# Two transformer blocks on one core: where the weights and the upper tiles begin, modulo 128 bytes

## The chip, the cores and the metric

The kernel runs on 1 of the 8 cores of a Trainium2 chip. The metric is the device time of one execution in microseconds, lower is better. The core has a matrix engine (TensorE, PE in the profile, its weight loads PEld), three engines for elementwise work (VectorE is DVE, ScalarE is ACT, GpSimd is POOL) and a queue for transfers (SyncE, SP). They share the on-chip memory SBUF (128 partitions, tiles are columns of bytes in each) and are ordered by semaphores that the kernel sets by hand. Matrix products go to the eight banks of PSUM (`ps`).

## The reference

A sequence of 512 tokens, 1024 wide, float32, passes through three layers. Cut to the order of the work:

```python
for i in range(2):                               # first block: NSA mixer, then sliding-window mixer
    mod = silu(c) @ ada_w[i] + ada_b[i]          # six vectors: sh1, sc1, g1, sh2, sc2, g2
    h = rms_norm(x, g) * (1 + sc1) + sh1
    y = nsa_mixer(h, ...) if i == 0 else swa_sink_mixer(h, ...)
    x = x + (1 + g1) * rms_norm(y, g)
    h = rms_norm(x, g) * (1 + sc2) + sh2
    y = relu(h @ w_up) ** 2 @ w_down             # 1024 -> 4096 -> 1024
    x = x + (1 + g2) * rms_norm(y, g)
x = x + hybrid_mixer(rms_norm(x), ...)           # second block: pooling and gated linear attention
x = x + memory_cross_attention(rms_norm(x), rms_norm(mem), wq, wkv, wo)
x = x + conv_ffn(rms_norm(x), ...)               # 1024 -> 2 x 2816 -> 1024
return rms_norm(x)
```

All matrix products are float32.

## The kernel before

**Products.** Every weight matrix is cut into units of 1024 x 128 elements (DC = 8 blocks of 128 x 128), 309 units in all, in one order of use. A unit is loaded by SP into a ring of four slots, `raw`. ScalarE rounds it to the fast float type of TensorE, `wh` (line 2540), and POOL writes the remainder, `wl = raw - wh` (line 802). The activations are split in the same way into a high and a low half: `ah`/`al`, `hh`/`hl`, `fh`/`fl`, `oh`/`ol`, `mh`/`ml`, `xoh`/`xol`. A float32 product is then three fast ones for each of the 8 blocks (lines 909, 910, 911 in `products`): `wh` by high, `wl` by high, `wh` by low. In these the weights are the stationary operand (128 columns) and the activations the moving one (512 tokens). `gemm_first` (lines 972, 973, 977) does the same for the first three units of a stage, block by block; `chunks` (1030 to 1032) for a part of a unit. `gemm_pairs` (957 to 959) and `last_values` (1510 to 1512) turn the roles around: 128 tokens of the activations are stationary and two units of weights move (2 x 128 columns); `compress` (1313 to 1315) as well, with 124 stationary columns that step by 496 bytes. For the 256 tokens of the memory the moving operand `mh` has 256 columns.

**Stages.** nsa_in (43 to 172 us in the trace), attention of NSA (to 349), nsa_out (to 404), mlp0 (to 774), swa_in (to 840), sliding-window attention (to 900), swa_out and mlp1 (to 1309), mix_in with pooling and gated linear attention (to 1449), mix_out and the products of the memory (to 1529), cross attention (to 1614), xo (to 1660), ffn (to the end). In the MLPs blocks of eight units alternate: up on `ah`, down on `hh`. In ffn up takes `fh`, down takes `hh`.

**Order.** Each engine runs its own program, written out by hand. TensorE waits for `lo_done` (POOL's wl) before a unit and for `evac` (the bank has been read); ScalarE may overwrite a slot of `wh` when TensorE has done with it (`unit_used`); SP loads into `raw` when POOL has done with the slot.

**Places.** `at(name, kib, shape)` puts a tile at `sb0 + kib * 1024` bytes of each partition. `sb0` is the first free byte rounded up to 64; here it is 16512, a multiple of 128. The lower tiles have whole KiB: `x` 0, `ah` 16, `al` 32, `y` 48 (also `xol`, `pr`, `me`), `raw` 64, `wh` 80, `wl` 96, then `rs`, `tt`, `sq` and the table of small inputs `sm` at 126, whose columns are listed in SMALL (2689 of them). Behind the table lie small tiles, `ident_r` and `mask_r` (the identity and two masks for the attention scores, made by the copies of lines 1799 to 1801 from columns of the table), and from `w0` on the upper region, which the stages use in turn: `hh` at w0, `hl` w0 + 16, `fh` w0 + 48, `fl` w0 + 32, `oh` w0, `ol` w0 + 38, `mh` w0 + 16, `ml` w0 + 24, `xoh` w0 + 50, `qs`, `ks`, `vv`, `pt` and others, each at w0 plus a multiple of 128 bytes. The table's 10756 bytes end at s1 = 126 + 169/16 KiB, and w0 = s1 + 3 KiB = 139.5625 KiB, which is 64 bytes past a multiple of 128.

Of the kernel before, what the change touches and what calls it, by code (L numbers as in the profile page):

```python
# [7 lines left out]
F32R = mybir.dt.float32r  # L8
# [5 lines left out]
P = 128  # L14
D = 1024
S = 512
DC = D // P
SC = S // P
# [6 lines left out]
KB = 1024  # L25
NEG = -1.0e30
RING = 4


UNITS_NSA_IN = 21  # L30
# [16 lines left out]
for _name, _count in STAGES:  # L47
# [2 lines left out]
UNITS = _n  # L50


SMALL = (("ones", P), ("ident", P), ("diag", P), ("prev", P), ("cmp_add", SC * P),
         ("inv", 1), ("cT", DC), ("ada_b", 96), ("norm_g", 64), ("pe", 32), ("b1", 4), ("b2k", 1), ("b2v", HD),
         ("w2", 4 * HD), ("sinks", HEADS), ("norm_mix", DC), ("norm_xattn", DC), ("norm_mem", DC),
         ("norm_ffn", DC), ("norm_final", DC), ("pool_scale", 4), ("gk_b", 2), ("gla_norm", 1),
# [2 lines left out]
COL = {}  # L59
_n = 0  # L60
for _name, _count in SMALL:
    COL[_name] = (_n, _n + _count)
    _n += _count
SMALL_COLS = _n
# [174 lines left out]
def over_units(eng, a, b, one):  # L239

    while a < b and (a % RING or b - a < 2 * RING):
        one(a, a % RING)
        a += 1
    turns = max(0, (b - a) // RING)
    if turns > 0:
        with eng.Fori(0, turns) as it:
            for slot in range(RING):
                one(it * RING + (a + slot), slot)
    for u in range(a + turns * RING, b):
        one(u, u % RING)  # L250


def build(nc, src, out):
# [4 lines left out]
    def at(name, kib, shape, dt=F32):  # L258

        return nc.alloc_sbuf_tensor_at(name, shape, dt, offset=sb0 + int(kib * KB))  # L260
# [12 lines left out]
    al = at("al", 32, [P, DC, S], F32R)  # L273
    y = at("y", 48, [P, DC, S])
    raw = at("raw", 64, [P, RING, DC, P])
    wh = at("wh", 80, [P, RING, DC, P], F32R)
    wl = at("wl", 96, [P, RING, DC, P], F32R)
    rs = at("rs", 112, [P, 2, S])
    tt = at("tt", 116, [P, 3, S])
    sq = at("sq", 122, [P, 2, S])  # L280
    sm = at("sm", 126, [P, SMALL_COLS])
    s1 = 126 + (SMALL_COLS * 4 + 63) // 64 / 16
    sxx = at("sxx", s1, [P, P])
    k1 = s1 + 0.5
    mod = at("mod", k1, [P, 96])
# [3 lines left out]
    warm = at("warm", k1 + 0.90625, [P, 1])  # L289
    neg_sinks = at("neg_sinks", k1 + 0.9375, [P, HEADS])  # L290
    ident_r = at("ident_r", k1 + 1, [P, P], F32R)
    mask_r = at("mask_r", k1 + 1.5, [P, 2, P], F32R)
    w0 = k1 + 2.5
    assert w0 + 68 <= 207.75, w0

    def small(name):
# [16 lines left out]


    pair = at("pair", w0, [P, 4, S])
    acc_in = at("acc_in", 112, [P, 1024])
    rot_h = at("rot_h", w0 + 12, [P, 2, 2, S], F32R)
    rot_l = at("rot_l", w0 + 20, [P, 2, 2, S], F32R)
    vv = at("vv", w0 + 28, [P, 2, SC, 4 * HD])
    pair_c = at("pair_c", 48, [P, 4, S])  # L320
    vtmp = at("vtmp", w0 + 36, [P, 2, S])
    ada_in2 = at("ada_in2", 116, [P, 2, 1024])
    xb_h = [at(f"xb_h{i}", (w0 + 44, 48)[i], [P, 16, 4 * NCMP], F32R) for i in range(2)]
    xb_l = [at(f"xb_l{i}", (w0 + 52, w0 + 36)[i], [P, 16, 4 * NCMP], F32R) for i in range(2)]
    hp = at("hp", 124, [P, 2, 2 * P])
    gate_t = at("gate_t", 56, [P, S])
    v_t = at("v_t", w0 + 44, [P, S])
    h1 = at("h1", w0 + 60, [P, 2, 2, 4 * NCMP])
# [8 lines left out]
    x2 = at("x2", 48, [P, 2, 4, S])  # L337
    ang = at("ang", 48, [P, 6, S])
    pos_i = at("pos_i", 60, [P, S], I32)
    trig = at("trig", 112, [P, 2, S])  # L340

    qs = at("qs", w0 + 16, [P, 4, S], F32R)
    ks = at("ks", w0 + 8, [P, 2, 2, S], F32R)
# [2611 lines left out]
def lay_out(i):  # L2955
# [24 lines left out]
    for what, n in (("u", 0), ("u", 1), ("d", 0), ("u", 2), ("d", 1), ("d", 2)):  # L2980
# [28 lines left out]
        quarter=np.arange(P)[:, None] == 32 * np.arange(4)[None, :], invcnt=np.broadcast_to(counts, (P, 64)), tri=np.where(np.arange(P)[:, None] % 64 <= np.arange(HD)[None, :], 1.0, 0.0))  # L3009
    table = np.concatenate([np.asarray(parts[name], dtype=f) for name, _ in SMALL], axis=1)  # L3010
    assert table.shape == (P, SMALL_COLS)
# [23 lines left out]
```

## Time and profile before

| | us |
|---|---|
| median of three runs | 2047.81 |
| all runs | 2047.92, 2042.06, 2047.81 |
| span of the profiled execution | 2041.0 |
| TensorE busy | 1973.7 (97%) |
| its weight loads | 1617.8 (79%) |
| VectorE busy | 1131.7 (55%) |
| POOL busy | 945.6 (46%) |
| ScalarE busy | 701.7 (34%) |

The span runs from the first to the last instruction of one profiled execution. That execution's own time is not given beside it; the runs lie 1 to 7 us above the span. Matmuls overlap their neighbours in the pipeline, so that a busy share of TensorE or the mean duration of a matmul doesn't say how fast they follow each other; the starts do.

### The profile page before, as it was taken

The numbers are of one execution on the slowest core, as the hardware profiler recorded it, in microseconds if no ns is written. First come the engines' busy times: TensorE is split into PE (matmuls) and PEld (weight loads), VectorE is DVE, ScalarE is ACT, GpSimd is POOL, SyncE is SP. The second block draws the span as 40 slices with busy tenths as digits, with TensorE's granted clock in tenths as the row PEclk, the third lists the DMA queues.
The fourth block names the chain that finished last, engine by engine and source line by source line (L and its number), as shares of the span: only waits on it lengthen the run. The fifth ranks groups of instructions, "written<-read, shape, count | busy, mean of one in ns | idle before, by whom it ended". The sixth has DMA issues, their size and how long they took to land.

```text
span 2041.0 us, 27018 instructions
## 1 busy us (share of the span) xinstructions
PE 1973.7 (97%) x10293; PEld 1617.8 (79%) x10293; DVE 1131.7 (55%) x1747; ACT 701.7 (34%) x1225; POOL 945.6 (46%) x552
## 2 busy tenths in 40 slices
PE   6998999999999999999999999999999999999997
PEld 5888777778888887877888888788797788888885
DVE  7675775973545567766322314686453368345163
ACT  3353654432222233654222213342443342222222
POOL 1465553465444445554544444542373244444442
PEclk9998999999999999999999999999999999999998
DMA  7765331545555524721332233221342223333331
GB/s 290 240 216 165 113 102 48 200 163 188 195 176 196 170 68 130 207 88 52 114 98 99 93 96 101 63 83 63 103 145 83 71 70 118 93 93 99 97 93 62
DMA packets 79989, 252.22 MB, mean 124 GB/s; under 512 B 12160, under 2 KB 12672, under 8 KB 79616
## 3 DMA queue, kind: packets, MB, share of 16 engines
q1 hardware_dynamic: 79872, 250.61, 38.0%
q8 instruction: 79, 1.29, 0.3%
q14 instruction: 38, 0.31, 0.0%
HBM read 235.21 MB, written 15.37 MB: 123 GB/s over the span
## 4 chain that ended last, share of the span: by engine, by line
PE 73%; issue 12%; POOL 7%; DVE 5%; ACT 3%; POOLq 0%; DVEq 0%; ACTq 0%
PE ps L909 20%; PE ps L911 20%; PE ps L910 20%; POOL wl L802 6%; PE ps L1195 2%; PE ps L1135 2%; ACT pr L2687 2%; PE ps L1167 1%; PE ps L1472 1%; DVE st L1947 1%; PE ps L1497 1%; POOL al L858 1%; PE ps L977 1%; POOL x L850 1%; PE ps L957 0%
## 5 line engine op out<-in xcount | busy, mean ns | idle before, releaser
L802 POOL TENSOR_TENSOR wl<-raw,wh 128x1024 fp32r<-128x1024 f32 x309 | 770.9, 2501 | 946.9 <-ACT wh L2540 946.7
L2540 ACT CAST wh<-raw 128x1024 fp32r<-128x1024 f32 x309 | 322.3, 1050 | 905.7 <-PE ps L911 840.5
L909 PE MATMUL ps<-ah,wh 128*128 128x512 f32 x904 | 357.7, 396 | 1.5 <-DVE pair L1877 1.5
L910 PE MATMUL ps<-ah,wl 128*128 128x512 f32 x904 | 352.8, 390 | 0.0
L911 PE MATMUL ps<-al,wh 128*128 128x512 f32 x904 | 352.6, 390 | 0.0
L909 PE MATMUL ps<-hh,wh 128*128 128x512 f32 x688 | 270.7, 393 | 1.9 <-DVE hl L2488 1.7
L911 PE MATMUL ps<-hl,wh 128*128 128x512 f32 x688 | 270.3, 393 | 0.0
L910 PE MATMUL ps<-hh,wl 128*128 128x512 f32 x688 | 268.0, 390 | 0.0
L909 PEld LDWEIGHTS ps<-ah,wh 128*128 128x128 f32 x904 | 170.1, 188 | 40.2 <-issue 2.6
L910 PEld LDWEIGHTS ps<-ah,wl 128*128 128x128 f32 x904 | 170.2, 188 | 36.3 <-issue 1.5
L911 PEld LDWEIGHTS ps<-al,wh 128*128 128x128 f32 x904 | 170.1, 188 | 36.0
L909 PEld LDWEIGHTS ps<-hh,wh 128*128 128x128 f32 x688 | 129.3, 188 | 30.5 <-DVE hl L2488 3.2
L910 PEld LDWEIGHTS ps<-hh,wl 128*128 128x128 f32 x688 | 129.2, 188 | 28.9
L911 PEld LDWEIGHTS ps<-hl,wh 128*128 128x128 f32 x688 | 129.2, 188 | 28.7
L911 PE MATMUL ps<-fl,wh 128*128 128x512 f32 x328 | 129.0, 393 | 0.0
L910 PE MATMUL ps<-fh,wl 128*128 128x512 f32 x328 | 128.2, 391 | 0.0
L909 PE MATMUL ps<-fh,wh 128*128 128x512 f32 x328 | 127.9, 390 | 0.0
L2687 ACT ACTIVATE pr<-ps,st 128x512 f32<-128x512 f32 (+1 forms) x192 | 94.2, 504 | 56.0 <-DVE st L1947 46.0
L2109 DVE TENSOR_SCALAR rs<-ps 128x512 f32<-128x512 f32 x64 | 44.2, 690 | 114.9 <-PE ps L911 109.9
L821 POOL TENSOR_SCALAR pr<-pr,st,gates 128x512 f32<-128x512 f32 (+3 forms) x128 | 81.5, 654 | 56.4 <-DVE st L1975 56.2
L1135 PE MATMUL ps<-ks,qs 128*128 128x256 f32 (+3 forms) x384 | 88.4, 336 | 5.7 <-ACT pr L2687 3.7
L2122 DVE TENSOR_TENSOR y<-ps,y 128x512 f32<-128x512 f32 x32 | 22.1, 691 | 127.3 <-PE ps L911 127.3
(402 smaller groups left out, 3262.7 us busy)
## 6 DMA issues: line engine op xcount, KB each, us to landing
raw<-in_units SPq DMA_DIRECT2D x309, 512.0 KB, 3.5
ada_mlp<-in_ada SPq DMA_DIRECT2D x64, 512.0 KB, 3.6
ada<-in_ada SPq DMA_DIRECT2D x16, 512.0 KB, 15.7
qs<-qscr SPq DMA_DIRECT2D x32, 256.0 KB, 3.4
ada_in<-in_ada SPq DMA_DIRECT2D x16, 512.0 KB, 3.6
ks<-kscr SPq DMA_DIRECT2D x24, 256.0 KB, 4.4
x<-in_xT SPq DMA_DIRECT2D x1, 2048.0 KB, 13.5
qscr<-rot_h SPq DMA_DIRECT2D x16, 128.0 KB, 2.4
```

What stands on the lines that cost most here:

```text
L802: nc.gpsimd.tensor_tensor(wl[:, slot], raw[:, slot], wh[:, slot].bitcast(F32), ALU.subtract).then_inc(lo_done, 1)
L821: op = nc.gpsimd.tensor_scalar(o, o, st[:, 2, n % 4, i:i + 1], gates[:, i, c:c + 1], ALU.mult, ALU.mult)
L850: nc.gpsimd.tensor_tensor(x[:, c], y[:, c], x[:, c], ALU.add).then_inc(x_new_pool, 1)
L909: nc.tensor.matmul(out_ap, wh[:, slot, k], high[:, k0 + k], start=first and k == 0, stop=False)
L910: nc.tensor.matmul(out_ap, wl[:, slot, k], high[:, k0 + k], start=False, stop=False)
L911: mm = nc.tensor.matmul(out_ap, wh[:, slot, k], low[:, k0 + k], start=False, stop=last and k == ks - 1)
L1135: nc.tensor.matmul(o, qs[:, Q_SLOT[j], i * P:(i + 1) * P], ks[:, slot, part, k0 * P:k1 * P], start=part == 0, stop=False)
L1195: mm = nc.tensor.matmul(ps[HD * h:HD * h + HD, bank, q[0] * P:(q[-1] + 1) * P], vv[:, kind, kb, col_v:col_v + HD], pt[:, n[h] % 4, place[k ...
L2109: link(v.tensor_scalar(rs[:, k % 2], b, 0.0, None, ALU.max))
L2122: v.tensor_tensor(y[:, c], bank(), y[:, c], ALU.add).then_inc(evac, 1)
L2540: a.copy(wh[:, slot], raw[:, slot]).then_inc(hi_done, 1)
L2687: a.activation(pr[:, n % 3, b * S + col:b * S + col + width], ps[:, plan.s_bank(w, b), col:col + width], ACT.Exp, bias=shift[:, i:i + 1], ...
```

## The change

It moves tiles and does nothing else. PAD is 1/8 KiB, 128 bytes. `wh` and `wl` begin 64 bytes later (PAD / 2), `rs` to `sm` and the tiles behind them 128 bytes later. `mask_r` no longer has a tile of its own: it lies over the columns prev and diag of the table, from which it is made, and the two columns change places in SMALL so that their order is that of `mask_r`. That frees 1 KiB, and w0 becomes 139, a multiple of 128 bytes. So `wh` and `wl` go from 0 to 64 modulo 128, all that is placed from w0 goes from 64 to 0, `mask_r` from 64 to 0; `ah`, `al`, `y`, `raw`, `xol`, the table keep 0, and `ident_r` and `sxx` keep 64.

```diff
--- before.py
+++ after.py
@@ -25,6 +25,7 @@
 KB = 1024
 NEG = -1.0e30
 RING = 4
+PAD = 1 / 8
 
 
 UNITS_NSA_IN = 21
@@ -50,7 +51,7 @@
 UNITS = _n
 
 
-SMALL = (("ones", P), ("ident", P), ("diag", P), ("prev", P), ("cmp_add", SC * P),
+SMALL = (("ones", P), ("ident", P), ("prev", P), ("diag", P), ("cmp_add", SC * P),
          ("inv", 1), ("cT", DC), ("ada_b", 96), ("norm_g", 64), ("pe", 32), ("b1", 4), ("b2k", 1), ("b2v", HD),
          ("w2", 4 * HD), ("sinks", HEADS), ("norm_mix", DC), ("norm_xattn", DC), ("norm_mem", DC),
          ("norm_ffn", DC), ("norm_final", DC), ("pool_scale", 4), ("gk_b", 2), ("gla_norm", 1),
@@ -273,13 +274,13 @@
     al = at("al", 32, [P, DC, S], F32R)
     y = at("y", 48, [P, DC, S])
     raw = at("raw", 64, [P, RING, DC, P])
-    wh = at("wh", 80, [P, RING, DC, P], F32R)
-    wl = at("wl", 96, [P, RING, DC, P], F32R)
-    rs = at("rs", 112, [P, 2, S])
-    tt = at("tt", 116, [P, 3, S])
-    sq = at("sq", 122, [P, 2, S])
-    sm = at("sm", 126, [P, SMALL_COLS])
-    s1 = 126 + (SMALL_COLS * 4 + 63) // 64 / 16
+    wh = at("wh", 80 + PAD / 2, [P, RING, DC, P], F32R)
+    wl = at("wl", 96 + PAD / 2, [P, RING, DC, P], F32R)
+    rs = at("rs", 112 + PAD, [P, 2, S])
+    tt = at("tt", 116 + PAD, [P, 3, S])
+    sq = at("sq", 122 + PAD, [P, 2, S])
+    sm = at("sm", 126 + PAD, [P, SMALL_COLS])
+    s1 = 126 + PAD + (SMALL_COLS * 4 + 63) // 64 / 16
     sxx = at("sxx", s1, [P, P])
     k1 = s1 + 0.5
     mod = at("mod", k1, [P, 96])
@@ -289,8 +290,9 @@
     warm = at("warm", k1 + 0.90625, [P, 1])
     neg_sinks = at("neg_sinks", k1 + 0.9375, [P, HEADS])
     ident_r = at("ident_r", k1 + 1, [P, P], F32R)
-    mask_r = at("mask_r", k1 + 1.5, [P, 2, P], F32R)
-    w0 = k1 + 2.5
+    mask_r = at("mask_r", 126 + PAD + COL["prev"][0] / 256, [P, 2, P], F32R)
+    w0 = 139
+    assert k1 + 1.5 <= w0
     assert w0 + 68 <= 207.75, w0
 
     def small(name):
@@ -313,16 +315,16 @@
 
 
     pair = at("pair", w0, [P, 4, S])
-    acc_in = at("acc_in", 112, [P, 1024])
+    acc_in = at("acc_in", 112 + PAD, [P, 1024])
     rot_h = at("rot_h", w0 + 12, [P, 2, 2, S], F32R)
     rot_l = at("rot_l", w0 + 20, [P, 2, 2, S], F32R)
     vv = at("vv", w0 + 28, [P, 2, SC, 4 * HD])
     pair_c = at("pair_c", 48, [P, 4, S])
     vtmp = at("vtmp", w0 + 36, [P, 2, S])
-    ada_in2 = at("ada_in2", 116, [P, 2, 1024])
+    ada_in2 = at("ada_in2", 116 + PAD, [P, 2, 1024])
     xb_h = [at(f"xb_h{i}", (w0 + 44, 48)[i], [P, 16, 4 * NCMP], F32R) for i in range(2)]
     xb_l = [at(f"xb_l{i}", (w0 + 52, w0 + 36)[i], [P, 16, 4 * NCMP], F32R) for i in range(2)]
-    hp = at("hp", 124, [P, 2, 2 * P])
+    hp = at("hp", 124 + PAD, [P, 2, 2 * P])
     gate_t = at("gate_t", 56, [P, S])
     v_t = at("v_t", w0 + 44, [P, S])
     h1 = at("h1", w0 + 60, [P, 2, 2, 4 * NCMP])
@@ -337,7 +339,7 @@
     x2 = at("x2", 48, [P, 2, 4, S])
     ang = at("ang", 48, [P, 6, S])
     pos_i = at("pos_i", 60, [P, S], I32)
-    trig = at("trig", 112, [P, 2, S])
+    trig = at("trig", 112 + PAD, [P, 2, S])
 
     qs = at("qs", w0 + 16, [P, 4, S], F32R)
     ks = at("ks", w0 + 8, [P, 2, 2, S], F32R)
```

## Rows read from the trace of the kernel before

**Rows 1.** The page, busy us (share) xinstructions; granted clock in tenths over 40 slices

```profile
PE 1973.7 (97%) x10293; PEld 1617.8 (79%) x10293; DVE 1131.7 (55%) x1747; ACT 701.7 (34%) x1225; POOL 945.6 (46%) x552
...
PEclk9998999999999999999999999999999999999998
```

**Rows 2.** The chain that ended last, shares of the span by line

```profile
by line: PE ps L909 20.1%; PE ps L911 20.1%; PE ps L910 19.9%; issue 12.1%; POOL wl L802 5.5%; PE ps L1195 2.1%; PE ps L1135 1.9%; ACT pr L2687 1.6%; PE ps L1167 1.5%; PE ps L1472 0.8%; DVE st L1947 0.8%; PE ps L1497 0.7%; POOL al L858 0.6%
```

**Rows 3.** The page, costliest groups: xcount | busy us, mean ns | idle before

```profile
L802 POOL TENSOR_TENSOR wl<-raw,wh 128x1024 fp32r<-128x1024 f32 x309 | 770.9, 2501 | 946.9 <-ACT wh L2540 946.7
...
L909 PE MATMUL ps<-ah,wh 128*128 128x512 f32 x904 | 357.7, 396 | 1.5 <-DVE pair L1877 1.5
...
L909 PE MATMUL ps<-hh,wh 128*128 128x512 f32 x688 | 270.7, 393 | 1.9 <-DVE hl L2488 1.7
...
L909 PE MATMUL ps<-fh,wh 128*128 128x512 f32 x328 | 127.9, 390 | 0.0
```

**Rows 4.** Line 909, two stretches on ah: ns min/median/max, first to last start us

```profile
L909 PE MATMUL ps<-ah,wh x40: 389/389/389, 423.4 to 449.9; 128*128 128x512 f32 x40
...
L909 PE MATMUL ps<-ah,wh x64: 389/389/397, 1125.9 to 1168.8; 128*128 128x512 f32 x64
```

**Rows 5.** The same view, stretches on hh and on fh

```profile
L909 PE MATMUL ps<-hh,wh x63: 394/394/394, 1170.2 to 1212.7; 128*128 128x512 f32 x63
...
L909 PE MATMUL ps<-fh,wh x128: 388/388/388, 1793.8 to 1881.0; 128*128 128x512 f32 x128
```

**Rows 6.** The same view, a stretch on xoh

```profile
L909 PE MATMUL ps<-xoh,wh x43: 397/397/398, 1629.8 to 1659.2; 128*128 128x512 f32 x43
```

**Rows 7.** The timeline of TensorE, three triples on ah: start us, us, instruction

```profile
149.75 0.28 PE L957 MATMUL ps<-wh,ah 128*128 128x256 f32 x1
...
150.83 0.28 PE L957 MATMUL ps<-wh,ah 128*128 128x256 f32 x1
```

**Rows 8.** The timeline, three triples with mh moving

```profile
1501.80 0.28 PE L909 MATMUL ps<-mh,wh 128*128 128x256 f32 x1
...
1502.86 0.28 PE L909 MATMUL ps<-mh,wh 128*128 128x256 f32 x1
```

**Rows 9.** Lines 957 and 1510, mh as the weights: stretches, and three triples of each state

```profile
L957 PE MATMUL ps<-wh,mh x32: 276/276/286, 1508.9 to 1519.4; 128*128 128x256 f32 x32
...
1511.94 0.28 PE L957 MATMUL ps<-wh,mh 128*128 128x256 f32 x1
...
1512.96 0.28 PE L957 MATMUL ps<-wh,mh 128*128 128x256 f32 x1
...
L957 PE MATMUL ps<-wh,mh x16: 281/281/388, 1520.5 to 1525.9; 128*128 128x256 f32 x16
...
1523.80 0.28 PE L957 MATMUL ps<-wh,mh 128*128 128x256 f32 x1
...
1524.86 0.28 PE L957 MATMUL ps<-wh,mh 128*128 128x256 f32 x1
...
L1510 PE MATMUL ps<-wh,mh x7: 276/276/276, 1603.0 to 1605.1; 128*128 128x256 f32 x7
...
L1510 PE MATMUL ps<-wh,mh x7: 276/276/285, 1607.9 to 1610.0; 128*128 128x256 f32 x7
```

**Rows 10.** The groups of TensorE by shape: other products of 512 columns

```profile
L972 PE MATMUL ps<-ah,wh 128*128 128x512 f32 x144 | 58.5, 407 | 9.9 <-ACT ah L2599 7.3 <-ACT ah L2597 2.6
...
L909 PE MATMUL ps<-oh,wh 128*128 128x512 f32 x64 | 25.6, 400 | 0.7 <-DVE ol L2361 0.7
```

**Rows 11.** The chain in order of time, in nsa_in: start us, us, what

```profile
84.98 2.50 POOL wl L802
```

**Rows 12.** The span by windows: us, busy us (xinstructions) of each engine, PEclk, DMA, GB/s

```profile
900.00:1309.00 409.00, 405.58 (x1893) 332.45 (x1891) 151.72 (x224) 122.67 (x154) 188.11 (x82) 1.00 0.29 92
```

**Rows 13.** The groups of POOL by shape, the same subtraction into al and fl

```profile
L858 POOL TENSOR_TENSOR al<-y,ah 128x512 fp32r<-128x512 f32 x12 | 15.5, 1291 | 13.1 <-ACT y L2604 10.1 <-ACT ah L2597 3.0
...
L858 POOL TENSOR_TENSOR fl<-y,fh 128x512 fp32r<-128x512 f32 x3 | 3.9, 1298 | 4.9 <-ACT fh L2597 4.9
```

## The prediction

> **What bounds the kernel now.** I read the page first: the busy table says that TensorE works for 97% of a span of 2041.0 us, and the slices that it does so at a granted clock of mostly 9 to 10 tenths (2.4 GHz) [rows 1]. No other engine passes 55%. The chain of work that ended last puts 60% of the span on three lines, 909 to 911 [rows 2]. They are the three products of one step (k) of a matrix product: wh by the high half of the activations, wl by the same, wh by the low half. I call these three a triple. So the question is how fast triples follow each other.
>
> The mean durations of the groups (390 ns) can't tell that, since matmuls are pipelined [rows 3]. The starts can. The view of one line in a stretch gives its count with the first and the last start, so a pitch is (last - first)/(count - 1). Where do the tiles stand, modulo 128 bytes? Before, the lower tiles (ah, al, wh, wl) stand at 0, everything from w0 on (hh, hl, fh, fl, oh, ol, mh, ml, xoh) at 64, xol at 0 again. That sorts the same instruction into classes; W is the weights' (stationary) remainder, M that of the moving operand:
> - 512 columns, W0/M0 (ah): (1168.8 - 1125.9)/63 = 681 ns a triple, in another stretch 26.5/39 = 679.5; I take 680 [rows 4].
> - 512 columns, W0/M64: hh (1212.7 - 1170.2)/62 = 685.5; fh, the longest stretch, 87.2/127 = 686.6; I take 686.7 [rows 5].
> - 512 columns, W0 with a moving operand that changes between 64 and 0 (xoh, xol): 29.4/42 = 700 [rows 6].
> - 256 columns, W0/M0 (ah as weights, wh moving): 1.08/3 = 360 in the timeline [rows 7].
> - 256 columns, W0/M64 (mh moving): 1.06/3 = 353 [rows 8].
> - 256 columns, W64/M0 (mh as weights, wh moving): 10.5/31 = 339 over 32 triples, 1.02/3 = 340 in the timeline; but the 16 triples that follow on the same line, after a wait, keep 1.06/3 = 353. Their matmuls last 281 ns each, those of the 32 last 276; both stretches of line 1510, the same class, have 276, so the first state [rows 9].
>
> Shape, clock and engine are the same inside each size, so the start of the operands in memory is what is left. All exceed the bare streaming of the columns (3 x 512/2.4 = 640 ns, 320 ns for 256): W0/M0 by 40 at both sizes, W64/M0 by 20, or by 33 when it has settled in its second state.
>
> **The change, part by part.** After it the weights wh, wl stand at 64 and every other large tile at 0 (the assertion on w0 allows it: w0 = 139 KiB). All main triples become W64/M0. These are relative places: were the base itself 64 off, the class with weights in the shifted region and the moving operand in the lower one would still be that of rows 9.
>
> The program has 1056 triples on ah (904 on line 909, 144 in gemm_first, 8 in chunks), 1080 on hh, fh and oh (688 + 328 + 64), 64 on xoh (eight units of eight) [rows 3, 10]. 216 of those on ah belong to nsa_in and mix_in, where TensorE also waits for the POOL's wl, for gates and for scans; in the chain from 64 us on POOL wl stands with some 2.5 us for each unit [rows 11]. Half of their gain counts, so 1056 becomes 948. The rest is a stream with TensorE alone on the path: in the mlp stage of 900 to 1309 us it is busy 405.58 of 409 us [rows 12].
>
> With X as the triple at W64/M0 and 512 columns, the change of the time is 948 x (X - 680) + 1080 x (X - 686.7) + 64 x (X - 700) ns = 2092 X - 1431.1 us. Break-even is X = 684 ns.
>
> X itself is in no row: no 512-column product has W64/M0. From W0/M0 I see that 256 more columns for each matmul cost exactly their streaming, 320 ns a triple [rows 4, 7]; so 340 becomes 660, and the second state, 353.3, becomes 673.3. At W0/M64 the same step costs 333 (353.3 to 686.7), which would put 340 at 673 too. Of four entries into W64/M0 three settled at 340 (the first pair stretch and both of line 1510) and one at 353 [rows 9]. I take three streams at 660 and one at 673.3: X = 663.3, and 2092 x 0.6633 - 1431.1 = -43.4 us.
>
> Smaller terms: mh with 256 columns moving, 64 triples from 353 to about 343, -0.6 us. gemm_pairs on ah, 128 triples from 360 to the 353 of W0/M64, -0.9, half hidden: -0.4. gemm_pairs and line 1510 on mh become W0/M64, 64 triples from 343 to 353: +0.6. compress (32 triples): its weights step by 496 bytes, so they meet all remainders before and after: nothing.
>
> Attention: qs, ks, mask_r, vv, pt go from 64 to 0, ident_r stays. Lines 1195 and 1135 hold 4.0% of the chain, 82 us [rows 2]; a pitch that moved by 5% either way, the spread of rows 4 to 6 being 3%, gives at most 4 us, and I take 0.
>
> The other engines: POOL's subtraction takes 1291 ns into al at 0 and 1298 into fl at 64 [rows 13], so wl at 64 costs under 1% of 2.5 us; POOL is idle 947 us before it [rows 3], and ScalarE, which writes wh, is busy 34% of the span [rows 1]. That cover stays while a unit of eight triples takes 5.3 us against POOL's 2.5. The DMAs of raw don't move; a unit of 512 KB each 5.3 us is 99 GB/s beside 92 now over the mlp stage [rows 12]. mask_r now lies over prev and diag, which nobody reads afterwards: the same two copies in setup. The swap of diag and prev moves columns in one table: nothing.
>
> Sum: -43.4 - 0.6 - 0.4 + 0.6 = -43.8 us. The profiled span is 2041.0; the runs show 2042.06 to 2047.92, so 1 to 7 us lie around it; the page names no own time for the profiled execution. The sum is taken from the median, 2047.8: **2004 us**.
>
> One rule speaks against it. The Trainium skill, "SBUF — State Buffer", section "Who interferes with whom", says that TensorE has two independent read ports, one for the moving operand and one for weights, and never waits on anyone; where a tile starts would then change nothing, the rival of no effect below. The classes at 680, 686.7 and 700 ns [rows 4 to 6] contradict it here. The same skill, "TensorE: Matmul & The Clock Gate", section "Back-to-back issue gap", gives N/2.4 + 2.5 ns for one matmul, 647.5 ns a triple; by that as X the estimate would be 2092 x 0.6475 - 1431.1 = -77 us. The best class here stands 20 ns above bare streaming for three, not 7.5, so no row bears it out.
>
> **Rivals.**
> 1. All in the first state: X = 660 gives -50.2, about 1997 us. For it: three of four entries, 32 triples in a row.
> 2. All in the second, or an added column costs as at M64: X = 673.3 gives -22.5, about 2025 us. For it: the one entry after a stall; every block of the MLP is such an entry.
> 3. No effect: alignment isn't the cause, but the stage or what runs beside it: 2048. Against: hh and ah alternate in one stage, each block with its own pitch [rows 4, 5].
> 4. Slower: the offset weights cost at 512 columns what an offset moving operand does, or what the mixed class does. Its place is each switch from one matmul to the next, where the next weights are fetched beside the moving columns; X lies between 686.7 and 700, say 693, and gives +18.7, about 2066 us. It decides from X = 687 on (+0.3%). Against: rows 9, where W64 is the fastest class; for it: only 256 columns are shown there.
>
> **How the numbers follow.** Mixed states as forecast 0.45, rival 1 0.17, rival 2 0.18, rival 3 0.08, rival 4 0.07, and 0.05 for something that I don't see. Range: down to rival 1 with all of the discounted 216 triples (2.2), 4 us in attention and 4 of the runs' own spread, 1987; up to rival 2 with 4 us: 2030. That leaves out rivals 3 and 4 and the rest. A measurement of this kernel tells about 0.3% (6 us) from no change. Faster 0.83, same 0.09, slower 0.08.
>
> **What would show it.** In the profile after: the starts of line 909 on ah and on hh must have one and the same pitch, 660 or 673; equal at 680 or above means that the step from 256 to 512 columns was wrong. xoh must fall from 700 to that value, the pair triples on mh rise from 340 to about 353. The spans of the mlp stages must shrink by 2.5 to 3.5%, attention hardly; if attention moves by over 4 us, that term was wrong. The 2.5 us of POOL's wl must stay; if TensorE's idle time grows by waits for it, the cover was thinner than I said. A pitch in which 660 appears, with a time that hasn't fallen, would mean that something else had bound the streams.

## The result, and the profile after

The change makes the kernel slower: 2072.96 us (median of 4, 2071.74 to 2073.62) beside 2045.47 us before (2042.06 to 2047.92). The ratio is 1.0135, with a 95% interval of 1.0121 to 1.0149, so +27.5 us. 2004 us had been forecast, and the range ended at 2030.

The page of the changed kernel (lines of the code are two higher than before, so 911 to 913 are the three products):

```profile
span 2069.9 us, 27018 instructions
...
PE 2003.8 (97%) x10293; PEld 1616.3 (78%) x10293; DVE 1132.6 (55%) x1747; ACT 701.3 (34%) x1225; POOL 942.9 (46%) x552
...
PEclk9999999999999999999999999999999999999999
...
L804 POOL TENSOR_TENSOR wl<-raw,wh 128x1024 fp32r<-128x1024 f32 x309 | 768.0, 2491 | 978.6 <-ACT wh L2542 978.4
```

The span has grown by 28.9 us, the medians by 27.5, and TensorE's busy time by 30.1, the other engines' hardly: POOL's subtraction takes 2491 ns beside 2501 [rows 3], and its idle time, most of it ended by ScalarE's `wh` as before, has grown by 32 us. The granted clock is as before [rows 1]. The shares of the chain haven't moved either [rows 2], the three lines have only become longer:

```profile
by line: PE ps L911 20.3%; PE ps L912 20.1%; PE ps L913 20.1%; issue 12.2%; POOL wl L804 5.3%; PE ps L1197 2.0%; PE ps L1137 1.9%; ACT pr L2689 1.6%; PE ps L1169 1.5%; PE ps L1474 0.8%; DVE st L1949 0.8%; PE ps L1499 0.7%; POOL al L860 0.6%
```

The starts of line 911 show where the time comes from. Here are stretches on ah, hh, ah, xoh and fh: count, ns min/median/max, first and last start in us.

```profile
L911 PE MATMUL ps<-ah,wh x40: 393/396/398, 425.7 to 453.0; 128*128 128x512 f32 x40
...
L911 PE MATMUL ps<-hh,wh x64: 393/396/398, 1097.2 to 1141.3; 128*128 128x512 f32 x64
...
L911 PE MATMUL ps<-ah,wh x64: 393/396/398, 1142.0 to 1186.1; 128*128 128x512 f32 x64
...
L911 PE MATMUL ps<-xoh,wh x47: 393/393/398, 1650.0 to 1682.2; 128*128 128x512 f32 x47
...
L911 PE MATMUL ps<-fh,wh x128: 393/396/398, 1819.3 to 1908.2; 128*128 128x512 f32 x128
```

The pitch of a triple is (last - first)/(count - 1): 27.3/39 and 44.1/63 = 700 ns on ah, where it was 680 [rows 4]; 44.1/63 = 700 on hh and 88.9/127 = 700 on fh, where it was 686.7 [rows 5]; 700 on xoh as before [rows 6]. As forecast, all have one pitch. It isn't 660 or 673 but 700, the highest of the classes seen before.

The units with 256 moving columns, in turn two pairs on ah and two on mh as the weights:

```profile
L959 PE MATMUL ps<-wh,ah x32: 279/279/383, 148.9 to 159.9; 128*128 128x256 f32 x32
...
L959 PE MATMUL ps<-wh,ah x32: 276/276/363, 160.4 to 171.0; 128*128 128x256 f32 x32
...
L959 PE MATMUL ps<-wh,mh x31: 280/280/283, 1530.6 to 1541.2; 128*128 128x256 f32 x31
```

On ah 11.0/31 = 355 and 10.6/31 = 342 ns (353.3 and 340.0 once the stretch is under way; 360 before [rows 7]), on mh 10.6/30 = 353 (340 before for these two [rows 9]). With mh moving, where the prediction had 343, nothing has changed: 11.3/32 = 353, as before [rows 8].

```profile
L911 PE MATMUL ps<-mh,wh x33: 281/281/281, 1519.0 to 1530.3; 128*128 128x256 f32 x33
```

By the first starts of their products, the stages take (us; ffn up to TensorE's last matmul):

| | nsa_in | NSA attention | mlp0 | mlp1 | mix_in | ffn |
|---|---|---|---|---|---|---|
| before | 134.0 | 171.5 | 370.4 | 361.9 | 130.1 | 372.2 |
| after | 135.2 | 171.5 | 378.0 | 369.9 | 131.1 | 378.3 |
| e1_upper_only | 134.0 | 172.0 | 368.9 | 360.0 | 130.3 | 368.8 |

21.7 of the 28.9 us lie in the three stages of MLP and ffn.

### The profile page after: what moved, and what is told of

It reads as the page before. It is cut to its first block, busy times and chain, and to the rows that moved or that the text cites. A ratio compares the mean times of both kernels' runs of the same rounds, so it can differ in the third digit from the quotient of the medians.

```text
span 2069.9 us, 27018 instructions
## 1 busy us (share of the span) xinstructions
PE 2003.8 (97%) x10293; PEld 1616.3 (78%) x10293; DVE 1132.6 (55%) x1747; ACT 701.3 (34%) x1225; POOL 942.9 (46%) x552
## 4 chain that ended last, share of the span: by engine, by line
PE 73%; issue 12%; POOL 7%; DVE 5%; ACT 3%; POOLq 0%; DVEq 0%; ACTq 0%
PE ps L911 20%; PE ps L912 20%; PE ps L913 20%; POOL wl L804 5%; PE ps L1197 2%; PE ps L1137 2%; ACT pr L2689 2%; PE ps L1169 1%; PE ps L1474 1%; DVE st L1949 1%; PE ps L1499 1%; POOL al L860 1%; PE ps L979 1%; POOL x L852 1%; PE ps L974 0%
## 5 line engine op out<-in xcount | busy, mean ns | idle before, releaser
L804 POOL TENSOR_TENSOR wl<-raw,wh 128x1024 fp32r<-128x1024 f32 x309 | 768.0, 2491 | 978.6 <-ACT wh L2542 978.4
L911 PE MATMUL ps<-ah,wh 128*128 128x512 f32 x904 | 363.5, 402 | 0.8 <-DVE pair L1879 0.8
L912 PE MATMUL ps<-ah,wl 128*128 128x512 f32 x904 | 358.2, 396 | 0.0
L913 PE MATMUL ps<-al,wh 128*128 128x512 f32 x904 | 357.7, 396 | 0.0
L2111 DVE TENSOR_SCALAR rs<-ps 128x512 f32<-128x512 f32 x64 | 44.1, 689 | 123.8 <-PE ps L913 118.7
```

Of the source, the lines that this page charges most:

```text
L804: nc.gpsimd.tensor_tensor(wl[:, slot], raw[:, slot], wh[:, slot].bitcast(F32), ALU.subtract).then_inc(lo_done, 1)
L911: nc.tensor.matmul(out_ap, wh[:, slot, k], high[:, k0 + k], start=first and k == 0, stop=False)
L912: nc.tensor.matmul(out_ap, wl[:, slot, k], high[:, k0 + k], start=False, stop=False)
L913: mm = nc.tensor.matmul(out_ap, wh[:, slot, k], low[:, k0 + k], start=False, stop=last and k == ks - 1)
L2111: link(v.tensor_scalar(rs[:, k % 2], b, 0.0, None, ALU.max))
```

## The experiments

**The two halves of the change.** The first takes back the move of the weights, the second that of the upper region (the diffs are against the changed kernel).

```diff
-    wh = at("wh", 80 + PAD / 2, [P, RING, DC, P], F32R)
-    wl = at("wl", 96 + PAD / 2, [P, RING, DC, P], F32R)
+    wh = at("wh", 80, [P, RING, DC, P], F32R)
+    wl = at("wl", 96, [P, RING, DC, P], F32R)
```

> The change without the move of the weights: wh and wl stay at 0 modulo 128, the upper region at 0 as in the changed kernel. Theory after the result: the weights' 64 bytes alone made the loss (a triple of 512 columns at W64/M0 takes 700 ns), and the upper region's move is a gain. Then every triple is W0/M0, 680 ns on ah, hh, fh, oh and xoh, and the time is 1080 x 6.7 + 64 x 20 ns = 8.5 us under the kernel before, about 2037 us. Rival: the region's move is what costs (something in hh, qs, ks or pt), then this kernel is slower than before, up to 2073 us, and the triples on hh are over 686.7 ns.

Measured: 2035.77 us (5 runs) beside 2045.18, ratio 0.995 (0.9936 to 0.9964). It is faster than the kernel before and than the changed one. The starts on ah, hh and xoh:

```profile
L911 PE MATMUL ps<-ah,wh x64: 389/389/389, 1123.8 to 1166.6; 128*128 128x512 f32 x64
...
L911 PE MATMUL ps<-hh,wh x64: 389/389/389, 1167.3 to 1210.1; 128*128 128x512 f32 x64
...
L911 PE MATMUL ps<-xoh,wh x63: 389/389/397, 1613.4 to 1655.6; 128*128 128x512 f32 x63
```

42.8/63 = 679 ns on both ah and hh (to the tenth of a microsecond that the row gives), 680 on xoh. So the upper region's move is the gain that the formula gives, 1080 x 6.7 + 64 x 20 ns = 8.5 us, and the loss is the weights'.

```diff
-    w0 = 139
+    w0 = 139 + PAD / 2
```

> The change's other half: wh and wl at 64, the upper region at 64 again (w0 = 139.0625 KiB). ah becomes W64/M0 and hh, fh, oh W64/M64. Three theories for 512 columns. (a) Only the distance of the two operands counts: ah 700 ns a triple, hh 680, in all 19 - 7 = +12 us, about 2057. (b) The costs of the two sides add (20 ns for W64, 6.7 for M64): ah 700, hh 706.7, +41 us, about 2086. (c) Weights at 64 cost 20 ns whatever the other operand does: 700 for both, +33 us, about 2079.

Measured: 2054.39 us, ratio 1.0042 (1.0027 to 1.0058), so +9.2 us beside the +12 of reading (a), +41 of (b) and +33 of (c); the span, 2053.2, is 12.2 over that of before. (In the runs that are listed with both, the span is about 1.8 us under the run's own time. So the span of 2041.0 belongs to an execution of about 2043 us, one of the fastest of before, and the span of e2 to its slowest, 2055.01; the medians are the fairer pair.) Blocks on ah and hh:

```profile
L911 PE MATMUL ps<-ah,wh x64: 393/394/395, 1136.7 to 1180.8; 128*128 128x512 f32 x64
...
L911 PE MATMUL ps<-hh,wh x64: 388/390/396, 1181.5 to 1224.4; 128*128 128x512 f32 x64
```

ah, 64 bytes away from its weights, takes 44.1/63 = 700 ns. hh, which stands at 64 like its weights, takes 42.8/63, as if both were at 0. Where each operand stands doesn't matter; how far apart they are does.

**Everything 64 further.** The kernel of e1 with one line changed:

```diff
-    sb0 = (nc.sbuf_base + 63) // 64 * 64
+    sb0 = (nc.sbuf_base + 63) // 64 * 64 + 64
```

> The kernel of e1_upper_only with every tile 64 bytes further, so all are at 64 modulo 128 and the distances are those of e1. (a) Distance alone counts: 680 ns everywhere, about 2037 us. (b) Added costs: 706.7 everywhere, about 2092 us. (c) Weights at 64 cost 20 ns: 700 everywhere, about 2079 us.

Measured: 2035.51 us, ratio 0.9951 (0.9936 to 0.9966), e1's time. The longest stretch on fh:

```profile
L911 PE MATMUL ps<-fh,wh x128: 389/389/389, 1793.0 to 1879.4; 128*128 128x512 f32 x128
```

86.4/127 = 680 ns with all at 64. Readings (b) and (c) have fallen.

**The streams by themselves.** This kernel does nothing but triples in the kernel's form, one class after another; B, C and D are tiles 32, 64 and 96 bytes past A's place:

```python
for i in range(144):
    mm(ps[:, i // 24 % 8, 0:n], (V if i % 3 == 1 else W)[:, i // 3 % 8 * P:i // 3 % 8 * P + P],
       (L if i % 3 == 2 else M)[:, i // 3 % 8 * n:i // 3 % 8 * n + n], start=i % 24 == 0, stop=i % 24 == 23)
```

> No part of the reference: only streams of the kernel's triples (wh by high, wl by high, wh by low, eight blocks), 144 matmuls each after 24 to settle, with the weights at 0, 32, 64 or 96 bytes modulo 128 (tiles wA to wD) and the moving operand likewise (mA to mD), at 512 and 256 columns, and at 384 and 128 columns for 0 and 64. It measures the pitch of each class by itself. If the start of the operands is the cause, 512 columns show 680 ns a triple for A/A, 686.7 for weights A with moving C, 700 for C with A, and 256 columns 360, 353 and 340 or 353; if it is something in the stages, all are alike. (a) distance: C/C is as A/A; (b) added costs: C/C 706.7; (c) C/C 700. No forecast for 32 and 96.

The row of a class counts one of its three products. At 512 columns weights A with moving A, A with B, C with A, C with C; then C with A at 256:

```profile
L301 PE MATMUL ps<-mA,wA x48: 388/389/390, 39.8 to 71.8; 128*128 128x512 f32 x48
...
L304 PE MATMUL ps<-mB,wA x48: 392/396/398, 78.0 to 110.9; 128*128 128x512 f32 x48
...
L325 PE MATMUL ps<-mA,wC x48: 393/394/395, 349.9 to 382.8; 128*128 128x512 f32 x48
...
L331 PE MATMUL ps<-mC,wC x48: 388/389/390, 428.1 to 460.1; 128*128 128x512 f32 x48
...
L373 PE MATMUL ps<-mA,wC x48: 275/276/277, 818.0 to 834.0; 128*128 128x256 f32 x48
```

(71.8 - 39.8)/47 = 681 for the first and 701, 700 and 681 for the next three; the last, 256 columns of the very class that takes 700 at 512, has 16.0/47 = 340. From the starts of all 144 matmuls of a class, at 512 columns: 680.0 where both are at the same place (A/A, B/B, C/C, D/D), 686.6 where the moving operand is 64 ahead (A/C, B/D), 700 for 64 behind (C/A, D/B), 700 for 32 ahead and behind and for 96 ahead, 702.9 for 96 behind. The start of the operands is the cause, with nothing of the stages around it. At 384 columns 520 for equal places and for A/C, 530 for C/A; at 128 all four classes tried have 335.

**What the period is.** The same streams with the tiles at 0, 64, 128 and 192:

```diff
-        wh[c] = at(f"w{c}", 20 + 4.25 * i + i / 32, [P, 1024], F32R)
+        wh[c] = at(f"w{c}", 20 + 4.25 * i + i / 16, [P, 1024], F32R)
```

(and so for the other three)

> No part of the reference: the streams of m1_streams with the letters A, B, C, D now at 0, 64, 128 and 192 bytes, for the weights and for the moving operand. The runs so far leave two readings of the 686.7 and the 700 ns: the moving operand 64 ahead is cheap and 64 behind dear (sign), or the remainders count modulo 256 (64 against 192). By the sign weights A with moving D costs 686.7 or something new and weights D with moving A costs 700; modulo 256, A with D costs 700 and D with A costs 686.7, B with A still 700. If 128 is the true period, A with C shows 680. Any class under 680 would be a place for the tiles that beats the equal one.

At 512 columns A with moving B, A with C, A with D, weights B with moving A, D with A; then at 256 columns A with D and B with A:

```profile
L304 PE MATMUL ps<-mB,wA x48: 393/394/395, 78.0 to 110.2; 128*128 128x512 f32 x48
...
L307 PE MATMUL ps<-mC,wA x48: 389/393/405, 116.5 to 149.3; 128*128 128x512 f32 x48
...
L310 PE MATMUL ps<-mD,wA x48: 392/396/399, 155.6 to 188.5; 128*128 128x512 f32 x48
...
L313 PE MATMUL ps<-mA,wB x48: 393/395/395, 194.8 to 227.7; 128*128 128x512 f32 x48
...
L337 PE MATMUL ps<-mA,wD x48: 387/389/389, 504.3 to 536.6; 128*128 128x512 f32 x48
...
L358 PE MATMUL ps<-mD,wA x48: 275/277/277, 716.2 to 732.2; 128*128 128x256 f32 x48
...
L361 PE MATMUL ps<-mA,wB x48: 280/281/282, 735.4 to 752.0; 128*128 128x256 f32 x48
```

By (last - first)/47: 685, 698, 700, 700 and 687, then 340 and 353. D with A is 192 behind and costs what 64 ahead does, A with D is 192 ahead and costs what 64 behind does. So it is the distance from the weights to the moving operand modulo 256. The tiles also lie whole KiB and odd multiples of 256 bytes apart, so that at 512 columns distances of 64 and 320, of 128 and 384, and of 192 and 448 modulo 512 are among these streams, each pair with one pitch. A distance of just 256 modulo 512, the partner of 0, was never run. From all starts, in ns for a triple:

| moving - weights, modulo 256 | 512 columns | 256 columns |
|---|---|---|
| 0 | 680.0 (4 classes) | 360.0 (4) |
| 64 | 686.6 to 686.7 (4) | 353.3 to 353.4 (4) |
| 128 | 697.0 to 697.3 (4) | 355.9 to 356.1 (4) |
| 192 | 700.0 (4) | 340.0 (2) and 353.3 to 353.4 (2) |

At 256 columns the equal place, the cheapest at 512, is the dearest, and 192, the dearest at 512, can be the cheapest. At 192 bytes and 256 columns the two states of [rows 9] are both there, in one run.

**The period in the kernel.** The changed kernel with its weights 128 bytes up:

```diff
-    wh = at("wh", 80 + PAD / 2, [P, RING, DC, P], F32R)
-    wl = at("wl", 96 + PAD / 2, [P, RING, DC, P], F32R)
+    wh = at("wh", 80 + PAD, [P, RING, DC, P], F32R)
+    wl = at("wl", 96 + PAD, [P, RING, DC, P], F32R)
```

> The changed kernel with wh and wl 128 bytes up instead of 64: all tiles of the products then begin at a multiple of 128, but weights and moving operands are 128 apart modulo 256. If the period is 128, this is e1_upper_only again: 680 ns a triple, about 2036 us. If it is 256, as the streams show (697 ns at a distance of 128), then 948 x 17 + 1080 x 10.3 - 64 x 3 ns = +27 us on the kernel before: about 2072 us, as slow as the change.

Measured: 2070.93 us beside 2044.4, ratio 1.013 (1.0113 to 1.0147), +26.5 us where the table gave +27. Blocks on ah and fh:

```profile
L911 PE MATMUL ps<-ah,wh x64: 390/393/404, 1142.5 to 1186.4; 128*128 128x512 f32 x64
...
L911 PE MATMUL ps<-fh,wh x128: 390/393/404, 1818.6 to 1907.1; 128*128 128x512 f32 x128
```

43.9/63 = 697 and 88.5/127 = 697 ns. All tiles of the products begin at multiples of 128, and the kernel is as slow as the changed one.

**Mixed places.** In the streams of m5, each of the four tiles has a place of its own; the letters are wh, wl, high, low:

```python
W, V, M, L, n = wh["A"], wl["A"], mh["B"], ml["A"], 512
```

> No part of the reference: streams as in m5_mod256 with the four tiles of a triple (wh, wl, high, low) at places of their own, 0 (A), 64 (B), 128 (C) or 192 (D), for 512 and then 256 columns. It asks why xoh and xol (64, 64, 0 over weights at 0) took 700 ns in the kernel before, where the mean of 686.6, 686.6 and 680 is 684.4. If each matmul paid for the distance of its own two operands, AABA would show 684.4, ABAA (wl alone 64 up) 686.7, AAAB 682.2. If the switch between two distances costs by itself, these lie above, AABA at 700.

AABA and, as an example with all but wh at 64, ABBB:

```profile
L313 PE MATMUL ps<-mB,wA x48: 391/391/391, 196.3 to 228.9; 128*128 128x512 f32 x48
...
L331 PE MATMUL ps<-mB,wA x48: 389/391/393, 429.7 to 461.9; 128*128 128x512 f32 x48
```

32.6/47 = 694 and 32.2/47 = 685 ns. From all starts: AABA 693.3, ABAA 693.4, AAAB 695.9, AADA 703.3, AAAD 686.7, ABBB 686.6. The mean of the three distances would be 684.4 for AABA, 686.7 for ABAA and 682.2 for AAAB: there mixing costs 7 to 14 ns on top, but for AAAD, whose mean is 686.7, nothing. But the 700 of xoh and xol [rows 6], which is AABA, isn't reached; what else it needs wasn't tried.

**One side without a run of memory.** One operand is read as one element over and over:

```python
(V if i % 3 == 1 else W)[:, i // 3 % 8 * P:i // 3 % 8 * P + 1].to_broadcast([P, P])     # weights
(L if i % 3 == 2 else M)[:, i // 3 % 8 * n:i // 3 % 8 * n + 1].to_broadcast([P, n])     # moving
```

> No part of the reference: the streams of m5_mod256 with one or both operands read as one element over and over (a broadcast of the first column) instead of a run of memory, at equal places (weights A, moving A) and at the dear distance of 192 (A, D), 512 and 256 columns; and the plain streams at 0, 64, 128, 192 and 64 against 0 once more, in another order. If the 40 to 60 ns over 640 arise where the weights' read and the moving operand's read meet in memory, a broadcast on either side makes the distance irrelevant (A/A and A/D alike) and brings the triple towards 640. If they belong to one side alone (the moving run's start), only that side's broadcast removes the difference. If nothing changes, the cost isn't in the reads. The repeated plain classes should show 680, 686.7, 697, 700, 700 again.

At 512 columns: A with A, moving operand broadcast; A with A, weights broadcast; plain A with B; A with D, moving broadcast; A with D, weights broadcast:

```profile
L304 PE MATMUL ps<-mA,wA x48: 378/378/378, 78.2 to 108.7; 128*128 128x512 f32 x48
...
L307 PE MATMUL ps<-mA,wA x48: 396/396/396, 115.0 to 147.5; 128*128 128x512 f32 x48
...
L313 PE MATMUL ps<-mB,wA x48: 397/397/398, 190.2 to 223.1; 128*128 128x512 f32 x48
...
L322 PE MATMUL ps<-mD,wA x48: 378/378/378, 307.3 to 337.8; 128*128 128x512 f32 x48
...
L325 PE MATMUL ps<-mD,wA x48: 391/394/397, 344.0 to 376.7; 128*128 128x512 f32 x48
```

The moving operand as a broadcast brings the triple to 30.5/47 = 649 ns, at the distance of 0 and of 192 alike (650.0 from all starts), 10 over bare streaming. The weights as a broadcast bring 693.3 and 695.1: the distance has nearly ceased to count, but it isn't cheap. So at 512 columns the dear part needs a run of memory on the moving side, and how dear it is depends on the place of the weights; the expectation that either broadcast would bring the triple towards 640 held for one side only.

At 256 columns it is otherwise. A with A: plain, moving broadcast, weights broadcast.

```profile
L334 PE MATMUL ps<-mA,wA x48: 283/283/283, 455.9 to 472.8; 128*128 128x256 f32 x48
...
L337 PE MATMUL ps<-mA,wA x48: 275/275/275, 475.8 to 491.6; 128*128 128x256 f32 x48
...
L340 PE MATMUL ps<-mA,wA x48: 276/276/276, 494.7 to 510.6; 128*128 128x256 f32 x48
```

From all starts these are 360.0, 335.2 and 340.0 ns, and the two broadcasts have the same numbers for A with D. Here either one does away with the distance, and 335.2 is close to the 335 that every stream of 128 columns took.

When are the weights read? In m1_streams, A with A, the load of the next weights (PEld) begins with the matmul before it and takes 0.19 of the 0.23 us between two matmuls:

```profile
45.23 0.39 PE L301 MATMUL ps<-mA,wA 128*128 128x512 f32 x1
45.23 0.19 PEld L301 LDWEIGHTS ps<-mA,vA 128*128 128x128 f32 x1
45.46 0.39 PE L301 MATMUL ps<-mA,vA 128*128 128x512 f32 x1
```

So the two reads lie beside each other in time. That it is the distance to the next weights, and not to a matmul's own, is not shown: in a stream of triples both give the same three distances.

The plain classes repeat (680.0, 697.0, 700.1, 700.0), but A with B, 64 ahead, took 700.0 here instead of 686.7, with the same code at the same distance. So 64 too has a second state. What chooses it isn't shown: here the streams before it were broadcasts, and this run was on another chip than m1, m5 and m7, which all had 686.7, as had the kernel before in the stretches on hh, fh and oh that were read.

## Why the prediction was wrong

1. **What bounds the kernel, and where to look: right.** The time followed the pitch of the triples in all six whole kernels, and the classes of [rows 4, 5, 7, 8 and 9] came back in streams with nothing around them; the 700 of [rows 6] did not (693.3).
2. **The formula 2092 X - 1431.1: right, mostly somewhat large.** With X = 700 it gives +33.3 us; the span grew by 28.9, the medians by 27.5. For e1 it gives -8.5 (the medians -9.4), for e4 +27 (+26.5). Half of the gain was counted for the 216 triples of nsa_in and mix_in, 2.2 us; these stages moved by 1.2 and 1.0. (The 216 leave out the 24 of gemm_first in mix_in; the two stages have 240 on ah.) Of the 4.4 us of span that are missing, 2.5 lie in mlp0 and mlp1 (+7.6 and +8.0 for 8.5) and ffn (+6.1 for 7.2). The 24 triples of gemm_first in each of five stages were counted as stream, 0.5 us each, though they follow the norm with its waits. From its first start to the first start of the products behind it, mlp0, swa_in and mlp1 took 19.8 us and now take 19.9 to 20.0, mix_in went from 23.0 to 23.1 and ffn from 18.1 to 18.5: in four of the five the longer pitch is hidden, which makes about 1.6 us in all. The rest stays open. A slip in the sums: rival 1's 660 gives -50.4, not -50.2, and nothing hangs on it.
3. **X: the step that failed.** X was put at 663.3 and measured 700. The sum took 340 ns at 256 columns (weights 64 past the moving operand), added 320 for 256 more columns, "from W0/M0 I see that 256 more columns for each matmul cost exactly their streaming", and got 660. In that class 256 more columns cost 360: 340 at 256, 530 at 384, 700 at 512 in m1. That a surcharge stays the same with length was true of the one class it was read from, distance 0 (360, 520, 680 for 256, 384 and 512 columns), and of no other. The rows had warned: at the other distance 256 more columns had cost 333, and the forecast used that only as a rival, at 673. Both ends of the range were made of this one kind of step.
4. **The classes: half right.** They were told by each operand's remainder modulo 128. What counts is the difference, modulo 256. The rows of before couldn't tell this: they had W0 with M0 and M64, W64 with M0, but neither W64/M64 nor any distance of 128.
5. **Rival 4, at 7%, is what happened,** above its threshold (X = 687); 693 was taken from a bracket of 686.7 to 700, and it was the upper end. Its place, the next weights fetched beside the moving columns, fits the timeline of m1 and the broadcasts, but isn't proved by them. Rival 3, that the place has no effect, fell by m1 and by the result itself.
6. **The smaller terms.** Attention at 0, with a bound of 4 us: 0.0 for NSA, 0.1 for the sliding window (59.0 to 59.2 us from its first scores to the full units of swa_out). The subtraction's 2.5 us stayed, the cover held. gemm_pairs on ah went to 355 and 342 where 353 was said, those on mh to 353 as said, and mh moving stayed at 353 where about 343 was said, so that its 0.6 us didn't come. All are too small to matter. The rule of the Trainium skill, "SBUF — State Buffer", section "Who interferes with whom", that TensorE never waits on anyone and has two independent ports, doesn't hold here for its own two reads: 680 against 700 ns for the same triple, with nothing changed but the distance of the two operands.

## What to carry to other kernels

A pitch taken at one length of the moving operand can't be carried to another by adding the columns; where the class that a change makes isn't in the trace, the nearest row is a rival and not a price. For moving operands of 512 columns put weights and moving operands at the same remainder modulo 256 bytes (here 680 ns a triple against up to 703), and check the difference, not each address: a region aligned to 128, or both aligned to 64, says nothing. This doesn't carry to other lengths either: at 256 columns the equal place was the dearest (360 against 340 to 356), at 384 a distance of 64 was as good (520), at 128 it made no difference. Of this change the move of the upper region alone (e1_upper_only, 2035.8 us) is what to keep.

## What the runs showed of the hardware

- For float32r matmuls with a new weight load each, the pitch depends on (moving start - weights start) modulo 256: for 512 columns 226.7 ns at 0, 228.9 at 64, 232.3 at 128, 233.3 at 192, and 233.3 to 234.3 at odd multiples of 32 (32, 96, 160, 224). Moving all tiles by 64 bytes changed nothing (e1 and e3), and neither did the letter in the streams with equal places. Other offsets than multiples of 32 weren't run.
- The surcharge over bare streaming isn't constant with length: at a distance of 192 it is 6.7 ns a matmul for 256 columns and 20 for 512, at 0 it is 13.3 for 256, 384 and 512. At 128 columns every class tried has 111.7 ns, 58 over its bare streaming.
- Some distances have two states, each of which lasted for a whole stream: 113.3 or 117.8 ns a matmul at 192 with 256 columns (both in m5), 228.9 or 233.3 at 64 with 512 (m5 and m8), and in the changed kernel 117.8 and 113.3 at 64 with 256, in the first and the second pair of units on ah. Distance 0 had one in all streams. What chooses the state stays open.
- A moving operand that is a broadcast of one element runs at 216.7 ns for 512 columns and 111.7 for 256, at both distances tried (0 and 192).
